# A two-layer decoder on one core: unnormalised queries in the first layer, moved small steps, and a new deal of matmuls over the last steps of the second

## The reference, cut to what matters

```python
qkv = silu(causal_depthwise_conv(qkv, conv_w))
q = l2norm(q) * 128 ** -0.5;  k = l2norm(k)      # x * rsqrt(sum(x * x) + EPS), EPS = 1e-6
# chunked: lower = strict((k*beta) k^T * decay); solve (I + lower); attn = q k^T * decay
v_new = u - w @ S
o = (q * exp(g)) @ S + attn @ v_new
S = S * exp(g_last) + k_tail^T @ v_new
o = rmsnorm(o, o_norm) * silu(z)                 # over the 128 numbers of a head and token
```

## Time and profile before

| what | value |
|---|---|
| median of 3 runs | 1349.96 us (1349.78 to 1350.57) |
| the profiled execution | 1350.38 us, of which 1348.6 us is the span |
| TensorE matmuls | busy 1285.0 us, 95% |
| VectorE | busy 984.7 us, 73% |
| ScalarE, GpSimd | busy 699.8 us (52%), 577.7 us (43%) |
| first layer's loop, heads 1 to 5 | 73.8 us each |

### The profile page before, as it was taken

How to read it: one execution, slowest core, us unless ns; L and a number is a source line. 1 busy time by engine, 2 the same in 40 slices (tenths; PEclk the granted TensorE clock), 3 DMA queues, 4 the chain that set the end, 5 groups by cost and what they waited for, 6 DMA issues and landing times.

```text
span 1348.6 us, 18350 instructions
## 1 busy us (share of the span) xinstructions
PE 1285.0 (95%) x6829; PEld 1064.7 (79%) x6829; DVE 984.7 (73%) x1701; ACT 699.8 (52%) x1112; POOL 577.7 (43%) x380
## 2 busy tenths in 40 slices
PE   7997999999999999999997999999999999998997
PEld 5786888888787878878885778788787878786786
DVE  5587888979898889886339767787778777777413
ACT  6355446364637364453226556656566656665303
POOL 6533333333333333432125694646565464632300
PEclk9998999999999999999999999999999999999999
DMA  7210110211111021206215111222111111118503
GB/s 194 76 46 16 32 48 16 63 33 47 48 42 53 16 63 32 60 31 221 82 32 187 32 32 33 57 60 71 48 47 48 47 47 48 54 56 293 175 1 125
DMA packets 106858, 91.42 MB, mean 68 GB/s; under 512 B 3106, under 2 KB 92307, under 8 KB 106771
## 3 DMA queue, kind: packets, MB, share of 16 engines
q1 hardware_dynamic: 106770, 90.25, 22.1%
HBM read 66.65 MB, written 23.59 MB: 67 GB/s over the span
## 4 chain that ended last, share of the span: by engine, by line
PE 70%; DVE 13%; ACT 7%; issue 7%; POOL 2%; DMA 0%; DVEq 0%; SPq 0%; ACTq 0%
PE psum L526 21%; PE psum L681 17%; PE psum L695 5%; PE psum L2540 4%; PE psum L2514 3%; PE psum L2527 2%; DVE stick L2101 2%; DVE terms L1938 2%; PE psum L2425 2%; PE psum L543 2%; PE psum L654 2%; PE psum L2336 1%; DVE small_L L1923 1%; PE psum L2409 1%; PE psum L2446 1%
## 5 line engine op out<-in xcount | busy, mean ns | idle before, releaser
L526 PE MATMUL psum<-u_hi,w_hi 128*128 128x512 f32 x640 | 260.4, 407 | 4.1 <-DVE u_lo L1651 1.7
L526 PE MATMUL psum<-u_hi,w_lo 128*128 128x512 f32 x640 | 258.9, 404 | 0.0
L526 PE MATMUL psum<-u_lo,w_hi 128*128 128x512 f32 x640 | 257.8, 403 | 0.0
L493 POOL TENSOR_TENSOR w_lo<-w_raw,w_hi 128x1024 fp32r<-128x1024 f32 (+1 forms) x45 | 107.9, 2398 | 237.3 <-ACT w_hi L488 225.4
L526 PEld LDWEIGHTS psum<-u_hi,w_hi 128*128 128x128 f32 x640 | 120.9, 189 | 29.8 <-issue 4.3
L526 PEld LDWEIGHTS psum<-u_hi,w_lo 128*128 128x128 f32 x640 | 120.9, 189 | 24.1 <-issue 1.9
L526 PEld LDWEIGHTS psum<-u_lo,w_hi 128*128 128x128 f32 x640 | 121.1, 189 | 20.8 <-issue 0.5
L1793 DVE SCALAR_TENSOR_TENSOR late<-raw,cols,late 128x1024 f32<-128x1024 f32 x72 | 128.2, 1781 | 1.8
L623 POOL TENSOR_TENSOR w_lo<-w_raw_b,w_hi 128x512 fp32r<-128x512 f32 x40 | 58.4, 1462 | 113.0 <-ACT w_hi L607 113.0
L488 ACT ACTIVATE w_hi<-w_raw 128x1024 fp32r<-128x1024 f32 (+1 forms) x45 | 45.9, 1020 | 109.5 <-PE psum L526 109.3
L2101 DVE TENSOR_TENSOR_SCAN stick<-soft 128x1024 f32<-128x1024 f32 (+3 forms) x64 | 101.2, 1582 | 0.2
(11 more groups left out here) (312 smaller groups left out, 3297.2 us busy)
## 6 DMA issues: line engine op xcount, KB each, us to landing
w_raw<-in_a_w_in SPq DMA_DIRECT2D x33, 512.0 KB, 4.1
w_raw<-in_b_w_in SPq DMA_DIRECT2D x16, 512.0 KB, 5.3
w_raw_b<-in_b_w_in SPq DMA_DIRECT2D x16, 512.0 KB, 5.4
b_rows<-o_part SPq DMA_DIRECT2D x14, 512.0 KB, 3.8
o_rows<-o_part_a SPq DMA_DIRECT2D x12, 512.0 KB, 3.6
x_stage<-in_x SPq DMA_DIRECT2D x8, 512.0 KB, 7.4
out<-fin_o SPq DMA_DIRECT2D x8, 512.0 KB, 2.6
u_lo<-b_rows SPq DMA_DIRECT2D x7, 512.0 KB, 8.4
```

The lines of the kernel that those rows point to most:

```text
L493: G.tensor_tensor(lo_tiles(key), raw_tiles(key), hi_tiles(key).bitcast(F32), ALU.subtract).then_inc(lo_done, 1)
L526: mm = PE.matmul(psum[:, half], (w_hi, w_hi, w_lo)[part][:, buffer(key), k], (u_hi, u_lo, u_hi)[part][:, k, half * HALF:(half + 1) * HALF] ...
```

## The change

1. **Queries unnormalised.** `q` is neither squared for a sum of its own, nor summed, nor multiplied by a reciprocal root. `qT` is made from `conv` in one step, and the products `q k^T` take `conv` directly. Instead ScalarE squares `q` with the scale 128*sqrt(EPS) (`square_q`, in slot 5 for half 1 and in slot 13 for half 0), VectorE adds this to the squares of `o` (`add_q`, where `copy_o` stood), and the sum of that over the head, with EPS*EPS*128, gives the right rmsnorm. So the EPS of the norm of `q` is kept exactly.
2. **Output squares.** The copy of `o` with its weight is made by ScalarE behind its square. `sum_squares_o(t, 1)` goes from slot 0 to behind the products of slot 1 of the next `t`, with bank 5 for both halves; the last one goes behind `last_group(1)`. Its Ln and Exp go from slot 0 to slot 2.
3. **Table load** stands in slot 22 behind `v_new`, no longer behind the square of `q`.
4. **A low part:** `LO_AT[0]` goes from slot 17 to 18, behind `rhs` and `invT` there. **Two masks:** the level-1 masks of `Lb` go from slot 6 to slot 11.
5. **Second layer:** steps 6 and 7 get (0, 8) and (12, 20) products in place of (0, 2) and (15, 23); head 0 gets 12 products ahead of its first transposes of `v` in place of 6; VectorE takes the group that ends in step 7 ahead of `exponent` there.
6. `row_in` and `fin_in` are merged in `par_in`; buffers are placed anew.

```diff
-HI_AT, LO_AT = (16, 4), (17, 13)
+HI_AT, LO_AT = (16, 4), (18, 13)
+MASK_AT = 11
-STEP_FILL = ((12, 23), (10, 15), (9, 13), (8, 11), (0, 15), (0, 12), (0, 2), (15, 23))
-FIRST_FILL = 6
+STEP_FILL = ((12, 23), (10, 15), (9, 13), (8, 11), (0, 15), (0, 12), (0, 8), (12, 20))
+FIRST_FILL = (12,) + (6,) * (H - 1)
...
-                for l, at in enumerate((5, 6, LEVEL_AT[1] + 1, LEVEL_AT[2] + 1)):
+                for l, at in enumerate((5, MASK_AT, LEVEL_AT[1] + 1, LEVEL_AT[2] + 1)):
...
+            def square_q(h, half):
+
+                if half == 0:
+                    if h > 0:
+                        o_added.wait(act, h - 1, 1)
+                elif h > 1:
+                    o_added.wait(act, h - 2, 2)
+                silu_kq.wait(act, h, 2)
+                A.activation(q_sq_first[:, :] if half == 0 else q_sq_second[:, h % 2], conv[:, 0, half_range(half)],
+                             ACT.Square, scale=P * sqrt(EPS)).then_inc(q_sq_done.handle, 1)
...
                 A.activation(o_sq[:, :], psum[:, 3], ACT.Square).then_inc(osq_done.handle, 1)
+                if half == 1:
+                    og_done.wait(act, t, 1)
+                elif t > 0:
+                    og_done.wait(act, t - 1, 2)
+                A.activation(o_nrm[:, :], psum[:, 3], ACT.Copy, scale=cols[:, ONORM_COL:ONORM_COL + 1]
+                             ).then_inc(o_copied.handle, 1)
...
+                if s == 5:
+                    square_q(h, 1)
+                if s == 13:
+                    square_q(h, 0)
...
-                    if s == 0 and t >= 1:
+                    if s == 2 and t >= 1:
                         norm_scale(t - 1, 1)
...
                         else:
-                            norm_done.wait(dve, h - 1, 2)
-                            sq_ready.wait(dve, h - 1, 2)
+                            qg_done.wait(dve, h - 1, 1)
+                            gram_ready.wait(dve, h - 1, 4)
+                            q_sq_done.wait(dve, h - 1, 2)
...
-            def copy_o(t, half):
+            def add_q(t, half):
+
                 osq_done.wait(dve, t, half + 1)
-                V.tensor_scalar(o_nrm[:, :], psum[:, 3], cols[:, ONORM_COL:ONORM_COL + 1], None, ALU.mult
-                                ).then_inc(o_copied.handle, 1)
+                q_sq_done.wait(dve, t, 2)
+                V.tensor_tensor(o_sq[:, :], o_sq[:, :], q_sq_first[:, :] if half == 0 else q_sq_second[:, t % 2], ALU.add
+                                ).then_inc(o_added.handle, 1)
...
+                    if s == NC - 1:
+                        fill.to(STEP_AT[2 * s + 1])
                     exponent(*ahead)
...
-                    for n in range(2):
-                        if n == 1 and t >= 1:
-
-                            sum_squares_o(t - 1, 1)
-
-                        sq_lo_done.wait(pe, h, n + 1 if h > 0 else 2)
-                        for half in range(2):
-                            for i, part in enumerate((sq_hi[:, n], sq_lo[n][:, :])):
-                                mm = PE.matmul(psum[:, 4 + 2 * n + half], ones_r[:, :], part[:, half_range(half)],
-                                               start=i == 0, stop=i == 1)
-                        mm.then_inc(sums_ready.handle, 1)
...
+                        if bk == 4 and t >= 1:
+                            oln_done.wait(pe, t - 1, 2)
...
+                    if s == 1 and t >= 1:
+                        if t + 1 < H:
+                            ln_done.wait(pe, t + 1, 1)
+                        sum_squares_o(t - 1, 1)
```

More of the change, by code:

```diff
@@ L17 @@
 from contextlib import ExitStack
-from math import log
+from math import sqrt
 import concourse.bass as bass
@@ L947, in _ @@
             tok_ready.wait(sp, H - 1, 4)
-            norm_done.wait(sp, H - 1, 2)
+            qg_done.wait(sp, H - 1, 1)
+            norm_done.wait(sp, H - 1, 1)
+            q_sq_done.wait(sp, H - 1, 2)
             for k in range(HOME, KB):
@@ L1346, in norm_scale @@
                 osum_ready.wait(act, t, half + 1)
-                A.activation(o_rs[:, :], psum[:, 5 if half == 0 else 2], ACT.Ln, bias=eps_d[:, 0:1], scale=1.0 / P
+                A.activation(o_rs[:, :], psum[:, SUM_BANK], ACT.Ln, bias=eps_o[:, 0:1], scale=1.0 / P
                              ).then_inc(oln_done.handle, 1)
@@ L1431, in _ @@
             split_hi(("q", 1))
-            for n in (1, 0):
-                silu_conv(0, 1 - n)
-                square_kq(0, n)
+            for part_no in (0, 1):
+                silu_conv(0, part_no)
+            square_k(0)
+            A.preload_act_table_set(LN_EXP)
             split_hi(("k", 1))
@@ L1890, in recur @@
                 if s == 12:
-                    copy_o(t, 0)
+                    add_q(t, 0)
                 if s == 15:
@@ L2012, in _ @@
                     if s == 0 and t >= 1:
-                        copy_o(t - 1, 1)
+                        add_q(t - 1, 1)
                     if t + 1 < H:
@@ L2032, in _ @@
                         take(key, half)
-            copy_o(H - 1, 1)
+            add_q(H - 1, 1)
             for i in range(2):
@@ L2334, in sum_squares_o @@
             def sum_squares_o(t, half):
-                osq_done.wait(pe, t, half + 1)
-                PE.matmul(psum[:, 5 if half == 0 else 2], ones[:, :], o_sq[:, :], start=True, stop=True
-                          ).then_inc(osum_ready.handle, 1)
+                o_added.wait(pe, t, half + 1)
+                PE.matmul(psum[:, SUM_BANK], ones[:, :], o_sq[:, :], start=True, stop=True).then_inc(osum_ready.handle, 1)
             def recur(t, s):
@@ L2391, in prepare @@
                             inv_up[g].wait(pe, h - 1, LEVELS - 1)
-                    for n in range(2):
-                        if n == 1 and t >= 1:
-                            sum_squares_o(t - 1, 1)
-                        sq_lo_done.wait(pe, h, n + 1 if h > 0 else 2)
-                        for half in range(2):
-                            for i, part in enumerate((sq_hi[:, n], sq_lo[n][:, :])):
-                                mm = PE.matmul(psum[:, 4 + 2 * n + half], ones_r[:, :], part[:, half_range(half)],
-                                               start=i == 0, stop=i == 1)
-                        mm.then_inc(sums_ready.handle, 1)
+                    sq_lo_done.wait(pe, h, 1)
+                    for half in range(2):
+                        for i, part in enumerate((sq_hi[:, :], sq_lo_k[:, :])):
+                            mm = PE.matmul(psum[:, 4 + half], ones_r[:, :], part[:, half_range(half)],
+                                           start=i == 0, stop=i == 1)
+                    mm.then_inc(sums_ready.handle, 1)
                 if s == 2:
                     sum_in.wait(pe, h, 2)
-                    ln_done.wait(pe, h, 2)
+                    ln_done.wait(pe, h, 1)
                     for mask, bk in ((after[:, :], 6), (ones_r[:, :], 4)):
+                        if bk == 4 and t >= 1:
+                            oln_done.wait(pe, t - 1, 2)
                         for half in range(2):
```

127 lines of the change are left out of this document (59 added, 68 removed).

## The result

The changed kernel takes **1319.0 us** (median of 4 runs, 1318.2 to 1319.6) against 1349.9 us of before in the same comparison; the ratio is 0.977, with a 95% interval from 0.975 to 0.979. The profiled execution has a span of 1316.2 us, 32.4 less than before. The prediction was 1318, from the same 32.4.

What follows compares the result with a forecast made beforehand. TensorE was taken as the bound, busy 71.84 of 73.85 us a head, as long as VectorE keeps up. First layer -21.9 and second -10.5 sum to -32.4 from 1350.38: 1318 us, range 1308 to 1331.

Steps and rivals of the forecast that it cites:

- slot 0: First layer, turns 1 to 6: four matmuls and a wait go, output's sum returns behind slot 1; net 1.76 us each, -10.6.
- turns -1 and 0: First layer's first two turns: four matmuls go, and in turn 0 a wait for the low squares of `q`; -2.7 for both.
- last turn: Last turn of the first layer: a short wait goes, -0.3 us.
- slot 13: ScalarE's square of half of `q` ahead of `inv_first` makes TensorE wait 0.3 us in seven heads: +2.1.
- end of the layer: First layer's end: last output sum stands 2.8 us later behind two groups, partly covered by VectorE's adds; +0.8, an estimate.
- low part: Slots 17 to 18: `rhs` comes earlier, so TensorE's start about 1.0 us late goes in six heads; -6.3 with turn 6.
- masks: Slots 6 to 11: earlier `w_lo` removes TensorE's wait for `state`, 7 x 0.7 = -4.9 us.
- second layer: Steps 6 and 7: waits for `exponent` and a take shrink, `exponent` itself staying; 1.75 us in six transitions, -10.5.
- Masks on `invT`: Both masks block VectorE in slots 11 and 12, TensorE waits 1.0 more in slot 13: +7, 1325; chance 0.12.
- Waits of VectorE that come back: Shorter head leaves VectorE less slack, waits for `rhs` and `state` stay: 11.2 less gained, 1329; chance 0.10.
- New deal that moves its wait: Second layer: TensorE arrives earlier at the next `exponent` or take; the 10.5 shrink to 2, 1326; chance 0.08.
- The clock: Around 109 us the 0.50 clock stretch is shorter or absent: up to 3.4 us more gained, 1314; chance 0.10.

Runs made afterwards that it cites:

- run 4: Changed kernel with the low part back in slot 17, masks back in slot 6 and the second layer as before, together: 1340.4 us against 1350.1 of before.
- run 1: Changed kernel with the low part of the gated output back from slot 18 to slot 17, ahead of `rhs`: 1325.6 us.
- run 2: Changed kernel with the level-1 masks back from slot 11 to slot 6: 1325.7 us.
- run 3: Changed kernel with the second layer's old product numbers and VectorE's take of p5 behind `exponent` again: 1327.5 us.
- run 11: Changed kernel with an extra unused GpSimd product of 128x160 ahead of each of the two masks in slot 11: 1319.3 us.
- run 6: Changed kernel with the square of half 0 of `q` behind `inv_first` in slot 13, not ahead of it: 1317.1 us.
- run 7: Changed kernel with the rounding of the squares of `k` behind `v_new` in slot 22, not ahead of it: 1315.2 us.
- run 5: Changed kernel with the last output sum back ahead of the last groups of the first layer: 1320.5 us.
- run 8: Changed kernel with (14, 21) products in step 0 of the second layer in place of (12, 23): 1316.0 us.
- run 12: Changed kernel with the new product numbers in steps 6 and 7, but VectorE's take of p5 behind `exponent` again: 1326.1 us.
- run 9: Changed kernel with `q`'s square behind `inv_first`, rounding of `k`'s squares behind `v_new`, (14, 21) products in step 0, last output sum behind one group: 1309.7 us.

## Why the prediction was right, and where its terms were off

| term | predicted | measured |
|---|---|---|
| slot 0, turns -1 and 0, last turn, slot 13, end of the layer | -10.7 | -9.7 (run 4) |
| low part | -6.3 | -6.6 (run 1) |
| masks | -4.9 | -6.7 (run 2) |
| second layer | -10.5 | -8.5 (run 3) |
| sum | -32.4 | -31.5 by parts, -30.9 as a whole |

- **Slot 0** came as worked out, about 0.2 a head too small: run 4 has a head 1.3 us shorter than before, with 0.35 lost in slot 13 and 0.35 in slot 23, so 2.0 in place of 1.76. The output's sum cost 0.86 and not 0.97. Of the 3.2 us that a head lost, four matmuls are 0.93; the rest is waits and refilling. The Ln of the output sum fits in slot 2 with no wait, as assumed.
- **The low part** was right in place and price, and its cover too: the low part itself runs in 0.68 us now and delays nobody.
- **The masks** were right in place and 1.8 us too small. The mis-sized term is "7 x 0.7": a middle turn gains 0.8, turn 6 gains 1.5, and turn -1, where I gave them nothing, gains 0.5 us at its first `inv_first`. Wrong on the way was that the earlier `w_lo` falls on operations that it does not stretch. It also falls on the copy `small_T`, which took 0.22 us before and 1.72 now:

```profile
364.81 2.41 POOL L496 TENSOR_TENSOR w_lo<-w_raw,w_hi 128x1024 fp32r<-128x1024 f32 x1 [1.89 <-ACT w_hi L491]
...
366.04 1.72 DVE L1949 COPY small_T<-own_col 128x128 f32<-128x128 f32 x1
...
368.99 0.18 DVE L1962 TENSOR_TENSOR terms<-row_L_t,small_T 128x24 f32<-128x24 f32 x1
```

  So the collision moved and got smaller, it did not go: from the start of this copy to `state` VectorE takes 3.78 us (366.04 to 369.82) in place of 4.78, the 1 us that I had taken, for another reason. The fear about the new place was too large: `invT` is not late at all. Run 11 shows that 0.9 us more would still be free.
- **Slot 13** was predicted at +2.1 and measured at 1.9 (run 6).
- **VectorE's work** fell by 3.5 us a head and not 2.4: I had left out the low part (1.22 to 0.68) and that the masks' move takes 0.6 from the operations beside GpSimd.
- **The end of the first layer**, +0.8 against the kernel before, is borne out in sign: from slot 3 of the last turn to the last product of head 0 of the second layer (L657) it takes 118.2 us in place of 116.7, with one more stretch at half clock, and 117.3 in run 7, which has none. But it is not the price of having moved the sum: in its old place it costs 0.9 more (run 5), since `add_q` had joined its chain. The step that I left out is that the waiting operation had got a new one ahead of it.
- **The second layer** was 2 us too good. The step "`exponent` itself stays", and with it nothing else moves, failed: TensorE, 1.8 us ahead, comes to `b_v` 0.42 us too early, in step 0 of the next head. Six of these are 2.5 us; run 8 gives back 3.0.
- **Not in the prediction:** the late `v_new` in slot 23, 0.35 a head (run 7). In the kernel before the same operations stood ahead of it:

```profile
421.31 2.01 ACT L1331 ACTIVATE late<-late 128x1024 f32<-128x1024 f32 x2
423.22 1.04 ACT L1323 ACTIVATE dec<-late 128x1024 f32<-128x1024 f32 x1
...
425.39 0.28 ACT L1378 ACTIVATE v_new<-psum 128x128 f32<-128x128 f32 x1
```

  From the first silu to the square of `k` it is 1.91 us here and 2.11 in the changed kernel (406.10 to 408.21), and on to `v_new` 4.08 and 4.30 in all. `square_k` now waits for both silus (`silu_kq` at 2) where it waited for that of `k` alone, so it can't start until the second has ended. That this wait is the cause is read from the rows and the code; no run had it alone. I had looked at what the edit took from ScalarE there and not at this count.
- **The rivals.** Masks on `invT`: its mechanism is there (run 11), its price is 0 here. Waits of VectorE that come back: no, but each comes back in full when its part is undone. New deal that moves its wait: true of half the edit (run 12), and not of the whole. The clock: half of it came. The stretch at 0.50 around 109 us lasts 3.4 us in place of 6.8 of the earlier trace rows, worth some 1.7, and a new one of 3.4 us at 689.5 takes that back.

So the closeness of 1318 to 1319 is partly luck: terms 1.8 too small and 2.0 too large cancel, and so do what slot 0 gave beyond its term and what slot 23 took. The separate runs bear out the signs of the low part, the masks, slot 13 and the second layer one by one; slot 0 and the end of the first layer are known together from run 4, and apart only from the traces.

## What to carry to other kernels

When TensorE is the bound, look at each wait by start, find the one operation that is late, and see what stands ahead of it on its engine; moving a piece of work that nobody waits for was worth 6 to 7 us twice here, with no arithmetic saved. When a wait is filled with work, ask where the engine arrives early next: the fill in step 6 was worth 1.4 us without the change of VectorE's order and 8.5 with it, and left 3 more in step 0. And an engine without slack at one place (ScalarE in slot 13) pays every microsecond put there, while the next place may take 0.9 for nothing.

## What the runs showed of the hardware

- GpSimd and VectorE hold each other up in both directions. Two masks of one size took 1.59 us in slot 11 (the row at 379.80 above) and 4.45 in slots 17 and 18, where VectorE's operations with SBUF inputs surrounded them (the tap of 3.30 us and those behind it):

```profile
398.20 4.45 POOL L1117 TENSOR_TENSOR Lb<-dec,level 128x256 f32<-128x256 f32 x2
```

  By the Trainium skill (SBUF — State Buffer, "SBUF: two separate sides") the pair of ports that GpSimd shares with a VectorE operation of two SBUF inputs is locked for a whole instruction by whoever starts first, and the other blocks; both rows and run 11 agree. The copy `small_T`, with one input, took 1.72 us beside `w_lo` (the row at 366.04) and 0.22 in the kernel before.
- The lower clock does not come with the wait alone. In the last groups of the first layer the changed kernel and run 7 have the same three long waits, starts 2.5, 1.9 and 3.2 us late. The changed kernel has the clock at 0.50 behind the first and the third; the other keeps 1.00 throughout, as this stretch of run 7 from its third wait on shows:

```profile
710.60:714.00 3.40, 2.53 (x10) 1.85 (x11) 2.63 (x5) 2.60 (x5) 0.81 (x1) 1.00 0.44 173
```

  What decides it stays open. The executions of one kernel differ in it too: those of run 9 by 2 us, with mean granted clocks of 0.993 to 0.998.
- A sum of squares in full float32 is listed as two matmuls 0.43 us apart. It costs TensorE 0.86 to 0.87 us where the matmuls run on around it (slot 1, and slot 13 by 398.95 to 400.05 less a product), and 0.96 where TensorE had waited ahead of it (slot 0: 429.67 to 431.56 less four sums).
